# Who rounds h, and what stands inside the modulation block: an edit of one engine's order in a two-layer hybrid trunk

## The chip, the cores and the metric

The kernel runs on 1 core of one Trainium2 chip. The metric is the device time of one launch in microseconds (us), the median of a few runs. Engines are named as in the profile: PE is TensorE (matmul), PEld its weight load, DVE VectorE, ACT ScalarE, POOL GpSimd, SP the engine whose queue issues the transfers.

## The reference, cut to what matters

Two layers of a streaming encoder trunk on 256 positions of width 1024, in fp32. Each layer is a half-step SwiGLU feed-forward, a block of four token mixers, and a second half-step SwiGLU feed-forward, each with a shift, a scale and a gate that come from a vector c:

```
mod = silu(c) @ ada_w[l] + ada_b[l]          # 1024 x 9216 weights a layer
u = x * (1 + scale) + shift
y = (silu(u @ w1) * (u @ w3)) @ w2           # 1024 x 5632 and 2816 x 1024 weights
x = layer_norm(alpha * x + 0.5 * gate * y)
```

The change touches the four feed-forwards. Everything else stands in the reference, but no part of it is edited.

## The kernel before, in words

**Split arithmetic.** Matmuls run on fp32r operands, so each fp32 value is split in two: a high part, the value rounded to fp32r, and a low part, the value less its high part. Each product is three matmuls: high by high, low by high, high by low (L674 to L676 for the way in, L698, L701 and L702 for the way out).

**A feed-forward** is 11 chunks (c = 0 to 10) of 256 hidden columns. A chunk has two hidden tiles of 128 columns (ft = 0 and 1). PE does, for chunk c: 48 matmuls into tile 0, 48 into tile 1, then in most chunks the sum of a modulation block (four small matmuls, or one of 128x512 for a gate), then 24 matmuls out, in the order (rows 0, ft 0), (rows 1, ft 0), (rows 0, ft 1), (rows 1, ft 1). In chunks 9 and 10 it first does only (rows 0, ft 0) and (rows 0, ft 1); chunk 9's other half is done in chunk 10.

**The other engines in chunk c.** ACT: silu of tile 0 (L1782), the high part of w_in for the next chunk's tile 0 (L1789), silu of tile 1, the high part of w_in's tile 1, a gate copy if there is one, the high parts of w_out for the next chunk (L1800). DVE, one instruction after the other in this order: the low parts of both w_out tiles (w_out_low, L1208); for each tile the product h (L1192), its high part by a copy (L1195), its low part (L1197), together ffn_tile, and then the low part of one w_in tile of the next chunk (w_in_low, L1203); then the modulation block. In chunk 0 both w_in_lows come after both tiles. An instruction of DVE that waits holds up all that are behind it in this order.

**The modulation block** (ada_block) is a vector by matrix product done on DVE: 8 steps of 128x512 (L1126 or L1129 first, then 7 of L1132), each of which multiplies one slice of the 2 MB buffer ada_w_sb (part of arena) by a value of silu(c) and adds it to an accumulator. There is one such buffer. SP issues the load of the next block (L346) when the last step of the block before it has counted acc_step. The blocks lie in chunks 0 to 9 of the first two feed-forwards, in chunks 0 to 4 and 7 to 9 of the third, and in 0 and 1 of the fourth. In each chunk SP first issues the next chunk's w_in (2 x 1 MB, L381, freed by PE's first matmul out) and w_out (1 MB, L389, freed by PE's last), then the block's load.

**Chunk 10 of the first and third feed-forward** is written out apart from ffn_chunk on DVE, with the same instructions; in those two feed-forwards some chunks are followed by steps of a rotation table (L1372 to L1378), and the high part of the last w_out waits for the last of these. The names that the change touches are ffn_tile and ffn_chunk of DVE and ffn_chunk of ACT.

Of the kernel before, what the change touches and what calls it, by code (L numbers as in the profile page):

```python
# [32 lines left out]
CHUNKS = D_FF // CW  # L33
# [48 lines left out]
ADA = {(0, 0): dict(zip(range(10), range(0, 10))), (0, 1): dict(zip(range(10), range(12, 22))),  # L82
       (1, 0): dict(zip((0, 1, 2, 3, 4, 7, 8, 9), range(22, 30))), (1, 1): dict(zip((0, 1), (30, 31)))}
# [24 lines left out]
def trunk(nc, x, c, ada_w, ada_b, ln_g, ln_b, ffn_w13, ffn_w2, w_in, w_out, sinks, w_uq, w_iq,  # L108
# [3 lines left out]
    with ctx:  # L112
# [946 lines left out]
        def _(v):  # L1059
# [55 lines left out]
            def ada_block(n, buf, loaded, count, ts=range(8), first=0):  # L1115

                acc = acc_of(n)


                v.wait_ge(sem(loaded), count * 16)  # L1120
                if acc_free(n) and ts[0] == 0:
                    v.wait_ge(sem("ada_summed"), acc_free(n))
                for t in ts:
                    if t == 0 and gate_of(n) is not None:
                        v.wait_ge(sem("gate_bias_loaded"), 16 * (gate_of(n) + 1))
                        v.scalar_tensor_tensor(acc[:, :], buf[:, t - first, :], cs[:, t:t + 1], gate_bias_row[:, :], ALU.mult, ALU.add  # L1126
                                               ).then_inc(sem("acc_step"), 1)
                    elif t == 0:
                        v.tensor_scalar(acc[:, :], buf[:, t - first, :], cs[:, t:t + 1], None, ALU.mult).then_inc(sem("acc_step"), 1)  # L1129
                    else:  # L1130
                        v.wait_ge(sem("acc_step"), n * 8 + t)
                        v.scalar_tensor_tensor(acc[:, :], buf[:, t - first, :], cs[:, t:t + 1], acc[:, :], ALU.mult, ALU.add  # L1132
                                               ).then_inc(sem("acc_step"), 1)
# [50 lines left out]
            def ffn_tile(ft, tile):  # L1184

                v.wait_ge(sem("silu_ready"), tile + (ft + 1))
                gate = PS[:, 5 + 2 * ft, 0:T] if tile % 22 == 0 else PS[:, 4 + ft, T:2 * T]
                ring, parts = h_ring, h_parts
                if tile % 22 == 20:
                    ring, parts = h_ring_last, h_parts_last  # L1190
                    v.wait_ge(sem("acc_step"), 8 * (10, 22, 30, 32)[tile // 22])
                v.tensor_tensor(halves2(ring[:, ft, :]), halves2(silu_ring[:, ft, :]), in_order(gate), ALU.mult  # L1192
                                ).then_inc(sem("h_step"), 1)
                v.wait_ge(sem("h_step"), tile * 2 + (2 * ft + 1))
                v.tensor_copy(parts[:, 2 + ft, :], ring[:, ft, :]).then_inc(sem("h_step"), 1)  # L1195
                v.wait_ge(sem("h_step"), tile * 2 + (2 * ft + 2))
                v.tensor_tensor(parts[:, ft, :], ring[:, ft, :], parts[:, 2 + ft, :].bitcast(F32), ALU.subtract  # L1197
                                ).then_inc(sem("h_done"), 1)

            def w_in_low(slot, ft, tile):  # L1200

                v.wait_ge(sem("w_in_high"), tile + 1)
                v.tensor_tensor(w_in_tile(w_in_lo, slot, ft), w_in_tile(w_in_ring, slot, ft), w_in_hi[ft][:, :, :, :].bitcast(F32),  # L1203
                                ALU.subtract).then_inc(sem("w_in_split"), 1)

            def w_out_low(slot, ft, tile):
                v.wait_ge(sem("w_out_high"), tile + 1)
                v.tensor_tensor(w_out_lo[slot][:, ft, :], w_out_ring[slot][:, ft, :], (w_out_hi_last if tile % 22 >= 20 else w_out_hi)[ft][:, :].bitcast(F32), ALU.subtract  # L1208
                                ).then_inc(sem("w_out_split"), 1)

            def ffn_chunk(l, f, c):

                slot = ff_group(f, c) % 2
                tile = ff_tile(l, f, c)
                by_tile = c == 0
                for ft in range(0 if by_tile else 2):
                    w_out_low(slot, ft, tile + ft)
                for ft in range(2):
                    if by_tile:
                        w_out_low(slot, ft, tile + ft)  # L1220
                    ffn_tile(ft, tile)
                    if c != CHUNKS - 1 and not by_tile:
                        w_in_low(1 - slot, ft, tile + (2 + ft))
                if by_tile:
                    for ft in range(2):
                        w_in_low(1 - slot, ft, tile + (2 + ft))
                if c in ADA[l, f]:
                    n = ADA[l, f][c]
                    ada_block(n, ada_w_sb, "ada_loaded", n + 1 if n < 10 else n - 1)

            def ada_pair(k):

# [511 lines left out]
        def _(a):  # L1744
# [34 lines left out]
            def silu_tile(ft, tile):  # L1779
                a.wait_ge(sem("ag_ready"), tile + (ft + 3))  # L1780
                a.wait_ge(sem("h_done"), tile + (ft + 1))
                a.activation(halves2(silu_ring[:, ft, :]), in_order(PS[:, 4 + (2 * ft if tile % 22 == 0 else ft), 0:T]), ACT.Silu).then_inc(sem("silu_ready"), 1)  # L1782

            def w_in_high(slot, ft, tile):

                a.wait_ge(sem("ag_ready"), tile + 1)
                if tile == 0:
                    a.wait_ge(sem("w_in_loaded0"), in_loads(0, 0))
                a.activation(w_in_hi[ft][:, :, :, :], w_in_tile(w_in_ring, slot, ft), ACT.Copy).then_inc(sem("w_in_high"), 1)  # L1789
# [12 lines left out]
            def ffn_chunk(l, f, c):  # L1802

                last = c == CHUNKS - 1
                slot = ff_group(f, c) % 2
                tile = ff_tile(l, f, c)
                for ft in range(2):
                    silu_tile(ft, tile)
                    if not last:
                        if ft == 0:  # L1810
                            a.wait_ge(sem(f"w_in_loaded{1 - slot}"), in_loads(l, ff_group(f, c + 1)))
                        w_in_high(1 - slot, ft, tile + (2 + ft))
                if not last:
                    if c - 1 in ADA[l, f] and gate_of(ADA[l, f][c - 1]) is not None:
                        copy_gate(ADA[l, f][c - 1])
                    w_out_high(l, f, c + 1)
                elif c - 1 in ADA[l, f] and gate_of(ADA[l, f][c - 1]) is not None:
                    copy_gate(ADA[l, f][c - 1])
# [26 lines left out]
            for l in range(DEPTH):  # L1845
# [171 lines left out]
                else:  # L2017
                    n = l * 3 + 2
# [220 lines left out]
```

## Time and profile before

| what | value |
|---|---|
| median of 3 runs | 1049.12 us (1047.61 to 1053.38) |
| profiled execution | 1054.62 us, its span 1052.8 us |
| PE busy | 1012.4 us, 96% |
| PEld busy | 896.1 us, 85% |
| DVE busy | 884.8 us, 84% |
| ACT busy | 431.5 us, 41% |
| POOL busy | 126.5 us, 12% |
| granted TensorE clock, mean | 0.982 |
| transfers | 250.85 MB, 238 GB/s |

A share is over the whole span. The four feed-forwards are at about 29 to 218, 356 to 534, 547 to 724 and 862 to 1036 us of it; the mixers and the layer norms are between them. All times in the rows below are counted from the start of the span.

### The profile page before, as it was taken

To read this page: it belongs to the slowest core of one execution; us is meant where nothing else is said; L and a number is where in the kernel's file an instruction comes from. 1 tells how busy PE (TensorE), PEld (TensorE's weight loads), DVE (VectorE), ACT (ScalarE), POOL (GpSimd) and SP (SyncE) were. 2 spreads that over 40 slices of the span, in tenths; PEclk is the share of its full clock that TensorE was granted. 3 is DMA by queue.
4 is the path that set the end of the run, shared out by engine and by line. 5 is a ranking of instruction groups with operands and counts; after the bars stand their busy time and mean duration, and the time that the engine had idled before them with its cause. 6 is when DMAs were issued, how large, how long until landed. Compare 5 with 4: busy or idle time off the path is not lost.

```text
span 1052.8 us, 17121 instructions
## 1 busy us (share of the span) xinstructions
PE 1012.4 (96%) x6905; PEld 896.1 (85%) x6905; DVE 884.8 (84%) x1381; ACT 431.5 (41%) x601; POOL 126.5 (12%) x196
## 2 busy tenths in 40 slices
PE   3999999999999999999999999999999999999997
PEld 2899998987875799999999999999787559999995
DVE  6999999978988899999979998997897678766665
ACT  0556433322463444444344643342237244443342
POOL 1015504003000000000000390310300000000000
PEclk9899999989999999999989999999998999999999
DMA  9999999852363689998957995997235247654641
GB/s 344 356 332 346 322 320 333 279 152 80 120 220 121 240 290 329 319 347 315 320 205 251 324 339 178 337 331 217 80 87 174 81 141 267 234 197 166 237 161 40
DMA packets 183882, 250.85 MB, mean 238 GB/s; under 512 B 21676, under 2 KB 131568, under 8 KB 183804
## 3 DMA queue, kind: packets, MB, share of 16 engines
q1 hardware_dynamic: 183804, 249.77, 69.7%
q8 instruction: 55, 0.90, 0.4%
q14 instruction: 23, 0.19, 0.1%
HBM read 248.70 MB, written 1.05 MB: 237 GB/s over the span
## 4 chain that ended last, share of the span: by engine, by line
PE 77%; DVE 12%; DMA 6%; issue 2%; ACT 2%; SPq 1%; POOL 0%; POOLq 0%; DVEq 0%; ACTq 0%
PE PS L676 11%; PE PS L675 11%; PE PS L674 10%; PE PS L797 9%; PE PS L698 5%; PE PS L701 5%; PE PS L702 5%; DMA arena<-in_ada_w_dram 4%; PE PS L882 3%; PE PS L1023 3%; PE PS L804 2%; DVE acc L1132 2%; DVE w_in_lo L1203 2%; DMA xn<-in_ada_w_dram 1%; PE PS L585 1%
## 5 line engine op out<-in xcount | busy, mean ns | idle before, releaser
L674 PE MATMUL PS<-u_hi,w_in_hi 128*128 128x256 f32 x1280 | 352.1, 275 | 0.0
L675 PE MATMUL PS<-u_lo,w_in_hi 128*128 128x256 f32 x1280 | 352.0, 275 | 0.0
L676 PE MATMUL PS<-u_hi,w_in_lo 128*128 128x256 f32 x1280 | 352.0, 275 | 0.0
L674 PEld LDWEIGHTS PS<-u_hi,w_in_hi 128*128 128x128 f32 x1280 | 245.6, 192 | 1.2
L675 PEld LDWEIGHTS PS<-u_lo,w_in_hi 128*128 128x128 f32 x1280 | 245.6, 192 | 1.0
L676 PEld LDWEIGHTS PS<-u_hi,w_in_lo 128*128 128x128 f32 x1280 | 245.8, 192 | 0.0
L1203 DVE TENSOR_TENSOR w_in_lo<-w_in_ring,w_in_hi 128x2048 fp32r<-128x2048 f32 x88 | 201.3, 2294 | 21.8 <-ACT w_in_hi L1789 21.8
L1789 ACT ACTIVATE w_in_hi<-w_in_ring 128x2048 fp32r<-128x2048 f32 x88 | 167.5, 1907 | 6.5 <-DMA w_in_ring<-in_ffn_w_dram 6.4
L1782 ACT ACTIVATE arena<-PS 128x256 f32<-128x256 f32 x88 | 33.7, 384 | 245.1 <-PE PS L676 233.9
L698 PE MATMUL PS<-w_out_hi,h_parts 128*128 128x512 f32 x320 | 127.0, 397 | 3.8 <-DVE h_parts L1197 3.8
L1800 ACT ACTIVATE w_out_hi<-w_out_ring 128x1024 fp32r<-128x1024 f32 x80 | 80.3, 1050 | 118.5 <-PE PS L702 118.5
L701 PE MATMUL PS<-w_out_lo,h_parts 128*128 128x512 f32 x320 | 121.3, 379 | 0.0
L702 PE MATMUL PS<-w_out_hi,h_parts 128*128 128x512 f32 x320 | 121.3, 379 | 0.0
L1208 DVE TENSOR_TENSOR w_out_lo<-w_out_ring,w_out_hi 128x1024 fp32r<-128x1024 f32 x80 | 95.5, 1231 | 9.6 <-ACT w_out_hi L1800 9.6
L1132 DVE SCALAR_TENSOR_TENSOR acc<-arena,cs,acc 128x512 f32<-128x512 f32 x126 | 95.5, 758 | 4.5
L797 PE MATMUL PS<-uT,w_in_ring 128*128 128x256 f32 (+1 forms) x416 | 95.0, 385 | 1.0 <-issue 1.0
L797 PEld LDWEIGHTS PS<-uT,w_in_ring 128*128 128x128 f32 (+1 forms) x416 | 77.7, 190 | 15.7 <-issue 4.7
L698 PEld LDWEIGHTS PS<-w_out_hi,h_parts 128*128 128x128 f32 x320 | 60.5, 189 | 17.7 <-issue 10.3
L1192 DVE TENSOR_TENSOR arena<-arena,PS 128x256 f32<-128x256 f32 x88 | 36.6, 416 | 44.2 <-ACT arena L1782 43.8
L701 PEld LDWEIGHTS PS<-w_out_lo,h_parts 128*128 128x128 f32 x320 | 60.6, 189 | 10.0 <-issue 2.8
L2076 POOL TENSOR_TENSOR rstd<-var_eps,neg_half 128x1 f32<-128x1 f32 x12 | 7.6, 631 | 505.4 <-DVE var_eps L1270 505.4
L702 PEld LDWEIGHTS PS<-w_out_hi,h_parts 128*128 128x128 f32 x320 | 60.5, 189 | 8.6
(343 smaller groups left out, 1368.4 us busy)
## 6 DMA issues: line engine op xcount, KB each, us to landing
w_in_ring<-in_ffn_w_dram SPq DMA_DIRECT2D x88, 1024.0 KB, 7.8
arena<-in_ada_w_dram SPq DMA_DIRECT2D x30, 2048.0 KB, 8.2
w_out_ring<-in_ffn_w_dram SPq DMA_DIRECT2D x44, 1024.0 KB, 7.0
w_in_ring<-in_w_in_dram SPq DMA_DIRECT2D x6, 1024.0 KB, 7.1
w_in_ring<-in_w_in_dram SPq DMA_DIRECT2D x10, 512.0 KB, 5.6
w_out_ring<-in_w_out_dram SPq DMA_DIRECT2D x4, 1024.0 KB, 6.5
w_in_ring<-in_w_in_dram SPq DMA_DIRECT2D x2, 2048.0 KB, 8.8
w_in_ring<-in_w_out_dram SPq DMA_DIRECT2D x4, 1024.0 KB, 6.8
```

The costliest lines, as they stand in the source:

```text
L674: pe.matmul(y, hi, u_moving(u_hi, kt), start=(i == 0), stop=False)
L675: pe.matmul(y, hi, u_moving(u_lo, kt), start=False, stop=False)
L676: mm = pe.matmul(y, lo[:, kt, half, :], u_moving(u_hi, kt), start=False, stop=(i == KT - 1))
L698: mm = pe.matmul(y, h_hi, moving_pairs(his[ft][:, cols]), start=(c == 0 and ft == 0), stop=False)
L701: pe.matmul(y, h_hi, moving_pairs(w_out_lo[slot][:, ft, cols]), start=False, stop=False)
L702: mm = pe.matmul(y, h_lo, moving_pairs(his[ft][:, cols]), start=False, stop=(c == CHUNKS - 1 and ft == 1))
L797: mm = pe.matmul(o[0:w, :], w_in_ring[(G_MIX + m) % 2][:, kt, c0:c0 + w], uT[:, kt, :], start=(i == 0), stop=(i == KT - 1))
L1132: v.scalar_tensor_tensor(acc[:, :], buf[:, t - first, :], cs[:, t:t + 1], acc[:, :], ALU.mult, ALU.add).then_inc(sem("acc_step"), 1)
L1203: v.tensor_tensor(w_in_tile(w_in_lo, slot, ft), w_in_tile(w_in_ring, slot, ft), w_in_hi[ft][:, :, :, :].bitcast(F32), ALU.subtract).then_i ...
L1208: v.tensor_tensor(w_out_lo[slot][:, ft, :], w_out_ring[slot][:, ft, :], (w_out_hi_last if tile % 22 >= 20 else w_out_hi)[ft][:, :].bitcast ...
L1789: a.activation(w_in_hi[ft][:, :, :, :], w_in_tile(w_in_ring, slot, ft), ACT.Copy).then_inc(sem("w_in_high"), 1)
L1800: a.activation((w_out_hi_last if c == CHUNKS - 1 else w_out_hi)[ft][:, :], w_out_ring[slot][:, ft, :], ACT.Copy).then_inc(sem("w_out_high" ...
```

## The change

DVE no longer makes the high part of h in chunks 1 to 9: ACT does (new function h_high), tile 0's after the high part of w_in's tile 0, tile 1's between silu of tile 1 and the high part of w_in's tile 1. In the time between h and its low part (h_low) DVE now does a low weight. In these chunks the low part of w_in's tile 0 is made in two halves (w_in_low_half). The low part of w_in's tile 1 moves from ahead of the modulation block to behind its third step. In chunk 10 of the second and fourth feed-forward, each w_out_low now stands just ahead of its own tile. Chunk 0, and chunk 10 of the other two, are as before. No PE or SP instruction changes.

```diff
                 v.tensor_tensor(halves2(ring[:, ft, :]), halves2(silu_ring[:, ft, :]), in_order(gate), ALU.mult
                                 ).then_inc(sem("h_step"), 1)
+                if 2 <= tile % 22 < 20:
+                    return
                 v.wait_ge(sem("h_step"), tile * 2 + (2 * ft + 1))
                 v.tensor_copy(parts[:, 2 + ft, :], ring[:, ft, :]).then_inc(sem("h_step"), 1)
+                h_low(ft, tile, ring, parts)
+
+            def w_in_low_half(slot, ft, tile, half):
+                kts = slice(4 * half, 4 * half + 4)
+                v.wait_ge(sem("w_in_high"), tile + 1)
+                ins = v.tensor_tensor(w_in_tile(w_in_lo, slot, ft)[:, kts], w_in_tile(w_in_ring, slot, ft)[:, kts],
+                                      w_in_hi[ft][:, kts, :, :].bitcast(F32), ALU.subtract)
...
-                for ft in range(0 if by_tile else 2):
-                    w_out_low(slot, ft, tile + ft)
-                for ft in range(2):
-                    if by_tile:
-                        w_out_low(slot, ft, tile + ft)
-                    ffn_tile(ft, tile)
-                    if c != CHUNKS - 1 and not by_tile:
-                        w_in_low(1 - slot, ft, tile + (2 + ft))
...
-                if c in ADA[l, f]:
-                    n = ADA[l, f][c]
-                    ada_block(n, ada_w_sb, "ada_loaded", n + 1 if n < 10 else n - 1)
...
+                w_out_low(slot, 0, tile)
+                ffn_tile(0, tile)
+                w_out_low(slot, 1, tile + 1)
+                h_low(0, tile)
+                w_in_low_half(1 - slot, 0, tile + 2, 0)
+                ffn_tile(1, tile)
+                w_in_low_half(1 - slot, 0, tile + 2, 1)
+                h_low(1, tile)
+                if n is not None:
+                    ada_block(n, ada_w_sb, "ada_loaded", loaded, range(3))
+                w_in_low(1 - slot, 1, tile + 3)
+                if n is not None:
+                    ada_block(n, ada_w_sb, "ada_loaded", loaded, range(3, 8))
...
+            def h_high(ft, tile):
+                a.wait_ge(sem("h_step"), tile * 2 + (2 * ft + 1))
+                a.activation(h_parts[:, 2 + ft, :], h_ring[:, ft, :], ACT.Copy).then_inc(sem("h_step"), 1)
...
                         if ft == 0:
                             a.wait_ge(sem(f"w_in_loaded{1 - slot}"), in_loads(l, ff_group(f, c + 1)))
-                        w_in_high(1 - slot, ft, tile + (2 + ft))
+                            w_in_high(1 - slot, ft, tile + (2 + ft))
+                        if c:
+                            h_high(ft, tile)
+                        if ft == 1:
+                            w_in_high(1 - slot, ft, tile + (2 + ft))
```

## Rows read from the trace of the kernel before

**Rows 1.** The page: busy time by engine; the chain that ended last, by engine.
```profile
PE 1012.4 (96%) x6905; PEld 896.1 (85%) x6905; DVE 884.8 (84%) x1381; ACT 431.5 (41%) x601; POOL 126.5 (12%) x196
PE 77%; DVE 12%; DMA 6%; issue 2%; ACT 2%; SPq 1%; POOL 0%; POOLq 0%; DVEq 0%; ACTq 0%
```

**Rows 2.** Stretches of one chunk each: length, then busy time and count by engine.
```profile
422.90:438.80 15.90, 15.90 (x121) 15.26 (x120) 14.62 (x19) 6.38 (x6) 0.00 (x0) 1.00 0.94 327
929.22:945.12 15.90, 15.90 (x121) 15.26 (x120) 9.70 (x11) 6.38 (x6) 0.00 (x0) 1.00 0.57 198
```

**Rows 3.** Waits of PE: us in total, times, the longest.
```profile
PE PS L698 <- DVE h_parts L1197: 3.8, 9, 0.7
PE PS L698 <- DVE h_parts_last L1197: 3.1, 3, 2.3
```

**Rows 4.** DVE in order of time, second feed-forward, chunk 4 (starts 438.80).
```profile
446.87 0.29 DVE L1195 CAST h_parts<-arena 128x256 fp32r<-128x256 f32 x1
451.94 2.29 DVE L1203 TENSOR_TENSOR w_in_lo<-w_in_ring,w_in_hi 128x2048 fp32r<-128x2048 f32 x1 [0.59 <-ACT w_in_hi L1789]
454.14 0.48 DVE L1129 TENSOR_SCALAR arena<-arena,cs 128x512 f32<-128x512 f32 x1
454.66 5.48 DVE L1132 SCALAR_TENSOR_TENSOR arena<-arena,cs 128x512 f32<-128x512 f32 x7
460.06 1.22 DVE L1208 TENSOR_TENSOR w_out_lo<-w_out_ring,w_out_hi 128x1024 fp32r<-128x1024 f32 x1
```

**Rows 5.** Issues of the modulation loads by SP, and their time to landing (us).
```profile
444.26 0.55 SPq L346 DMA_DIRECT2D arena<-in_ada_w_dram  x1
460.17 0.55 SPq L346 DMA_DIRECT2D arena<-in_ada_w_dram  x1
DMA to landing us min/median/max: 8.1/8.2/15.4
```

**Rows 6.** The first and the last of nine such issues in three feed-forwards; of four in the third.
```profile
59.42 0.55 SPq L346 DMA_DIRECT2D arena<-in_ada_w_dram  x1
189.82 0.55 SPq L346 DMA_DIRECT2D arena<-in_ada_w_dram  x1
...
380.73 0.55 SPq L346 DMA_DIRECT2D arena<-in_ada_w_dram  x1
508.72 0.55 SPq L346 DMA_DIRECT2D arena<-in_ada_w_dram  x1
...
570.42 0.55 SPq L346 DMA_DIRECT2D arena<-in_ada_w_dram  x1
618.14 0.55 SPq L346 DMA_DIRECT2D arena<-in_ada_w_dram  x1
```

**Rows 7.** The chain that ended last: its two longest waits for these loads.
```profile
138.95 11.16 DMA arena<-in_ada_w_dram
172.89 10.88 DMA arena<-in_ada_w_dram
```

**Rows 8.** DVE: blocks that waited for their load; what follows the first feed-forward's last block.
```profile
68.81 0.75 DVE L1126 SCALAR_TENSOR_TENSOR acc<-arena,cs,gate_bias_row 128x512 f32<-128x512 f32 x1 [0.51 <-DMA arena<-in_ada_w_dram]
69.61 5.48 DVE L1132 SCALAR_TENSOR_TENSOR acc<-arena,cs,acc 128x512 f32<-128x512 f32 x7
...
205.74 0.68 DVE L1372 TENSOR_TENSOR rot_flat<-sin_t,cos_t 128x512 f32<-128x512 f32 x1
...
579.91 0.49 DVE L1129 TENSOR_SCALAR qk_tanh<-arena,cs 128x512 f32<-128x512 f32 x1 [0.61 <-DMA arena<-in_ada_w_dram]
```

**Rows 9.** Around tile 1 of chunk 9 of the last feed-forward: DVE and PE.
```profile
1020.05 0.42 DVE L1192 TENSOR_TENSOR arena<-arena,PS 128x256 f32<-128x256 f32 x1 [1.26 <-ACT arena L1782]
1020.84 0.43 DVE L1197 TENSOR_TENSOR h_parts<-arena,h_parts 128x256 fp32r<-128x256 f32 x1
1021.41 0.45 PE L698 MATMUL PS<-w_out_hi,h_parts 128*128 128x512 f32 x1 [0.51 <-DVE h_parts L1197]
```

**Rows 10.** An ACT group: instruction, count, busy us, mean ns, idle before.
```profile
L1759 ACT ACTIVATE u_hi<-uT_lo 128x256 fp32r<-128x256 f32 x12 | 5.0, 417 | 0.4
```

More of the change, by code:

```diff
@@ L1193, in ffn_tile, with h_low @@
                                 ).then_inc(sem("h_step"), 1)
+                if 2 <= tile % 22 < 20:
+                    return
                 v.wait_ge(sem("h_step"), tile * 2 + (2 * ft + 1))
                 v.tensor_copy(parts[:, 2 + ft, :], ring[:, ft, :]).then_inc(sem("h_step"), 1)
+                h_low(ft, tile, ring, parts)
+            def h_low(ft, tile, ring=h_ring, parts=h_parts):
                 v.wait_ge(sem("h_step"), tile * 2 + (2 * ft + 2))
@@ L1198, in ffn_tile @@
                                 ).then_inc(sem("h_done"), 1)
+            def w_in_low_half(slot, ft, tile, half):
[3 more added lines that the diff above has]
+                                      w_in_hi[ft][:, kts, :, :].bitcast(F32), ALU.subtract)
+                if half == 1:
+                    ins.then_inc(sem("w_in_split"), 1)
             def w_in_low(slot, ft, tile):
@@ L1214, in ffn_chunk @@
                 tile = ff_tile(l, f, c)
-                by_tile = c == 0
-                for ft in range(0 if by_tile else 2):
-                    w_out_low(slot, ft, tile + ft)
-                for ft in range(2):
-                    if by_tile:
-                        w_out_low(slot, ft, tile + ft)
-                    ffn_tile(ft, tile)
-                    if c != CHUNKS - 1 and not by_tile:
-                        w_in_low(1 - slot, ft, tile + (2 + ft))
-                if by_tile:
-                    for ft in range(2):
-                        w_in_low(1 - slot, ft, tile + (2 + ft))
-                if c in ADA[l, f]:
-                    n = ADA[l, f][c]
-                    ada_block(n, ada_w_sb, "ada_loaded", n + 1 if n < 10 else n - 1)
+                n = ADA[l, f].get(c)
+                loaded = None if n is None else n + 1 if n < 10 else n - 1
+                if c in (0, CHUNKS - 1):
+                    for ft in range(2):
+                        w_out_low(slot, ft, tile + ft)
+                        ffn_tile(ft, tile)
+                    if c == 0:
+                        for ft in range(2):
+                            w_in_low(1 - slot, ft, tile + (2 + ft))
+                    if n is not None:
+                        ada_block(n, ada_w_sb, "ada_loaded", loaded)
+                    return
+                w_out_low(slot, 0, tile)
[9 more added lines that the diff above has]
+                w_in_low(1 - slot, 1, tile + 3)
+                if n is not None:
+                    ada_block(n, ada_w_sb, "ada_loaded", loaded, range(3, 8))
             def ada_pair(k):
```

## The prediction, on record before the changed kernel ran

> **What bounds the kernel now.** First the page's busy times and chain [rows 1]: PE is busy for 1012.4 of 1052.8 us and is 77% of the chain that ended last. The rest of the chain is mostly DVE (12%) and DMA (6%), so there are stretches that PE does not set. Then stretches of one chunk [rows 2]: where nothing delays PE, a chunk takes 15.90 us and PE is busy in all of it. No edit of DVE or ACT can make such a chunk shorter. In the second feed-forward DVE is busy for 14.62 us of the chunk, in the last one 9.70. Then PE's waits [rows 3]: all that PE loses to h is 3.8 us in nine waits and 3.1 in three. Their sum, 6.9 us or 0.7% of the span, is about all that this change can win.
>
> Last the loop between the modulation block and its load. There is one buffer, so the next load is issued when the last step is done (460.14; issue 460.17), and the next block can't start before it lands, 8.2 us later in the median [rows 4, 5]. In chunk 4 of the second feed-forward: issued 444.26, landed by 452.5, while DVE comes to the block at 454.14, after w_in_low of tile 1. The landing had 1.7 us to spare and nobody saw the load. In the first feed-forward the spare time is sometimes gone: two loads of 11.16 and 10.88 us stand in the chain that ended last [rows 7], and DVE waited 0.51 us before the block at 68.81 [rows 8]. There the loop is on the path that sets the end: its last block is followed by the rotation table, for which the last high w_out waits, and PE waits 2.3 us for h behind that [rows 3].
>
> **The change part by part.**
>
> *The copy of h leaves DVE.* It removes two copies of 0.29 us and a step of 0.04 each [rows 4], 0.66 us a chunk. ACT pays 0.42 us for the same shape [rows 10], twice a chunk; it is busy 6.38 of 15.90 us [rows 2], so this is hidden unless a tile waits for it. Cutting one w_in_low in two costs one more overlap of 0.08 us. DVE has 0.58 us less to do in each of 36 chunks. Where DVE is not on the path this is worth nothing.
>
> *h is low-rounded later.* In chunk 9 tile 1's product starts at 1020.05, its low part ends at 1021.27 and PE goes on at 1021.41 [rows 9]: 1.22 us on DVE, 0.14 to PE. Now half a w_in_low (1.22, the size of a w_out_low [rows 4]) stands between them: 0.42 + 1.14 + 0.35 = 1.91 us. (Each instruction starts 0.08 before its predecessor ends.) ACT's 0.42 fits under the half. So the low part of tile 1 is 0.7 us later where DVE was on time. In chunk 9 PE already waits, so it loses 0.7 more; that is so in three feed-forwards, and not in the first, where DVE is late. In chunks 1 to 8 PE asks for tile 1 six matmuls of 512 columns later. A chunk is 96 of 256 and 24 of 512 columns, 144 units in 15.90 us, so six are 1.33 us. Of these 0.5 to 0.67 were already used up, which leaves 0.66 to 0.8 against 0.7: nothing to 0.06 us a chunk. I take 0.06.
>
> *The fillers.* From the end of a block DVE now needs four pieces of 1.14, two of 0.34 and two of 0.35, 5.94 us, until tile 1's low part. PE wants it 13.3 us after the chunk's start (96 + 24 of the 144 units) less 0.15. So a block may end 7.2 us into the next chunk, later only where PE also sums a block. In [rows 4] it ended at 5.4: slack 1.8.
>
> *The low w_in moves into the block.* It is the same instruction, but before it stood ahead of the wait for the load, and filled the time until the landing. Now DVE comes to the wait 2.2 + 0.6 us earlier, finds the load not landed (1.7 us spare before), idles, and then does the low weight between landing and last step, which releases the next load. It lengthens the loop by 2.29 less 0.08 twice less the gap of 0.03 that it fills, 2.10 us. The block itself is 5.99 us (454.14 to 460.14), a gate's 6.26 (68.81 to 75.09) [rows 4, 8]. A round is now load + 0.06 + block + 2.10: with 8.2 us 16.35, with a gate 16.6, where PE's chunk is 15.90. Queued behind the wait are the rest of the block, tile 1's low w_in, and the whole next chunk of h; behind the last step waits SP with the next load. No queue of SP changes its order.
>
> The rule "Overlap DMA with compute" of the Trainium skill (DMA: Bandwidth & Descriptors, Rules for kernel authors) asks for an early issue and a late wait. Here the wait is made earlier and the next issue later. By that rule the edit is a loss; these rows agree as far as the 1.7 us go that were spare.
>
> **The sum.** In each feed-forward the rounds between two issues [rows 6] are set against the new ones.
>
> First: eight rounds took 189.82 - 59.42 = 130.4. New: eight loads of 8.2 and the known excess (9.4 by the block at 68.81, 11.16, 10.88: +6.9) are 72.5; 8 x 2.16 = 17.3; three gates and five others 48.7. That is 138.5, +8.1, and the last round 16.35 against 16.0 (205.82) makes +8.4. The two 11 us loads were slow because three others were under way; at a slower pace they should be quicker, at most by 5.7 in all. I take 1.5, so **+7.0**, all on the path. Bounds +2 to +10.
>
> Second: eight rounds took 128.0. New 8 x 10.36 + 48.7 = 131.6, +3.6 (3.3 with the 8.16 that most have). PE had about 1.8 of slack, but the two residual steps in chunks 2 and 8 (1.2 us each on DVE) stand in it, and chunk 9 adds up to 0.7. **+2.2**, bounds 0 to 4.
>
> Third: three rounds took 47.7. New 3 x 10.36 + 18.5 = 49.6, and the first load took 9.5 (570.42 to 579.91 [rows 6, 8]); a second one like it makes 52.2, +4.5. Blocks pause after chunk 4, with some 2.2 of slack there: +1.8; a PE wait of 0.65 in chunk 8 goes, chunks 9 and 10 add 1.1. **+2.2**, bounds 0 to 5.
>
> Fourth: only two blocks. 0.7 in chunk 9 and six times 0.06: **+1.1**, bounds 0 to 2.
>
> Together +12.5. Against the profiled execution's own 1054.62 us that is 1067.1. That execution lies 5.5 above the median of the runs; on the median, 1049.12 + 12.5 = **1061.6 us**. The bounds add up to +2 and +21.
>
> **The rivals.**
>
> *The relief wins (faster).* If the landings come before DVE does, the loop never closes, and DVE's 0.58 us a chunk is what counts: 9 x 0.58 = 5.2 us on the first feed-forward's path, where DVE and not the load stands most often, and PE's waits of 3.8 us [rows 3] go too, less 2.1 for chunk 9: some -5, 1044. For it: PE waits for h in twelve places, and ACT is 41% busy. [...] Against it: with DVE 2.8 us earlier at the wait and 1.7 spare, a load would have to take under 8.2 + 1.7 - 2.8 = 7.1 us, and the least is 8.1 [rows 5]. Its point of decision is a landing ahead of DVE. Chance 7%.
>
> *Given back (little change).* The loop is longer, but loads of the first feed-forward fall to 8.2 us when the pace slackens, and the others have enough slack: +2 there, +0.5 to +1.5 in each other one: +3 to +6, 1052 to 1055. For it: 5.7 us of excess in two loads. Chance 20%.
>
> *Loads stretch.* Each load now starts some 1.5 us later in its chunk and meets the 2 MB of w_in that follow PE's first matmul out; the transfer engines are 94% busy in the chunk of [rows 2]. At 9.4 us instead of 8.2 for 20 of the 27 loads: 24 us more on the loop, half of it hidden by slack: 1070 to 1078. The same sign has ACT's copy of tile 0, which stands behind a w_in_high that may wait for its own load. Chance 15%.
>
> **How the numbers follow.** The forecast has 58%. Its own range is 1056 to 1068. My 80% range is 1052 to 1070: it takes in most of the second rival and leaves out the first and most of the third. Less than 0.5% (5.2 us) can't be told from no change with a kernel of this spread. Faster by more: part of the first rival, 5%. Within: the rest of it, half of the second and a tail of the forecast, 15%. Slower: 80%.
>
> **What would show it.** Right: in the first three feed-forwards DVE idles before nearly every block for its load, 0.5 to 2 us (now 0.51 and 0.61, [rows 8]); issues of L346 lie 16.3 or 16.6 us apart or more, never 15.9; the low part of w_in tile 1 stands behind three steps, with the fourth step some 2.1 us after the third; the chain that ended last holds far more of DMA than 6%; PE's waits for h grow, the longest at the end of the first feed-forward; in the last feed-forward only chunk 9 is longer, with a wait of 1.2 to 1.4. Wrong: if DVE still comes to the blocks after the landings, or if the rounds of the first feed-forward stay at 16.3 on average.

## The result, and the profile after

The changed kernel is slower: 1065.49 us in the median (1063.79 to 1067.31) against 1048.55 (1047.61 to 1053.38) for the kernel before, a ratio of 1.0157 with a 95% interval of 1.0138 to 1.0177. That is 16.9 us. The forecast was 1061.6, so the sign and the range (1052 to 1070) held, and the size was 3.9 us short.

The page of the changed kernel, its busy times and its chain by engine, answers to [rows 1]:

```profile
PE 1015.1 (95%) x6905; PEld 892.1 (84%) x6905; DVE 859.1 (81%) x1345; ACT 459.5 (43%) x673; POOL 116.5 (11%) x196
PE 53%; DMA 19%; DVE 18%; issue 6%; ACT 1%; SPq 1%; POOL 0%; POOLq 0%; DVEq 0%; ACTq 0%
```

DVE has 25.7 us less to do, in 36 instructions less (0.58 us in each of 36 chunks, 20.9 us, had been worked out), and the program takes longer. PE's share of the chain fell from 77 to 53%, DMA's rose from 6 to 19%.

Now the modulation loads: the view of the one line that issues them, with who waited for them (us, times). First the kernel before:

```profile
  DVE acc L1126: 1.9, 3
  DVE qk_tanh L1129: 0.6, 1
```

The same view of the kernel after:

```profile
  DVE acc L1126: 11.2, 6
  DVE acc L1129: 8.4, 6
  DVE qk_tanh L1129: 7.7, 5
  DVE arena L1129: 3.9, 2
  DVE sig_o L1129: 1.4, 2
...
DMA to landing us min/median/max: 8.0/8.3/15.5
```

Four blocks waited 2.5 us in all before, 21 waited 32.6 us after. Three more blocks, each for a gate, waited for the small bias row that is issued right behind their load and landed 0.1 to 0.3 us after it:

```profile
DVE acc L1126 <- DMA gate_bias_row<-in_ada_b_dram: 6.7, 3, 2.4
```

So 24 of the 30 blocks waited, 39.3 us in all. The loads are as fast as they were: 8.3 us in the median against 8.2 [rows 5].

DVE in order of time in the second feed-forward, from the end of chunk 4 (it starts at 430.14) into chunk 5 (446.17); the loop that [rows 4] showed for the kernel before:

```profile
442.94 0.42 DVE L1203 TENSOR_TENSOR h_parts<-arena,h_parts 128x256 fp32r<-128x256 f32 x1
445.02 0.48 DVE L1129 TENSOR_SCALAR qk_tanh<-arena,cs 128x512 f32<-128x512 f32 x1 [1.66 <-DMA arena<-in_ada_w_dram]
445.54 1.54 DVE L1132 SCALAR_TENSOR_TENSOR qk_tanh<-arena,cs,qk_tanh 128x512 f32<-128x512 f32 x2
446.99 2.28 DVE L1218 TENSOR_TENSOR w_in_lo<-w_in_ring,w_in_hi 128x2048 fp32r<-128x2048 f32 x1
449.19 3.89 DVE L1132 SCALAR_TENSOR_TENSOR qk_tanh<-arena,cs,qk_tanh 128x512 f32<-128x512 f32 x5
453.00 1.22 DVE L1223 TENSOR_TENSOR w_out_lo<-w_out_ring,w_out_hi 128x1024 fp32r<-128x1024 f32 x1
```

SP's issues on either side of it:

```profile
436.48 0.55 SPq L346 DMA_DIRECT2D arena<-in_ada_w_dram  x1
453.12 0.55 SPq L346 DMA_DIRECT2D arena<-in_ada_w_dram  x1
```

Issued 436.48, landed after 8.51 us, first step at 445.02, last step done at 453.09, next issue 453.12: a round of 16.64 us. DVE idles for 1.66 us in front of the block, where the low weight stood before.

Stretches of one chunk each, as in [rows 2]: a plain one of the second feed-forward, chunk 2 of the third, a plain one and chunk 9 of the last:

```profile
446.17:462.21 16.04, 16.04 (x122) 15.18 (x120) 13.54 (x18) 7.21 (x8) 0.00 (x0) 1.00 0.90 310
586.55:606.45 19.90, 17.91 (x122) 16.60 (x121) 17.65 (x22) 10.07 (x12) 4.68 (x11) 0.91 0.93 320
956.49:972.52 16.03, 16.03 (x121) 15.17 (x120) 9.58 (x11) 7.10 (x8) 0.00 (x0) 1.00 0.58 197
1020.63:1035.37 14.74, 13.54 (x109) 12.91 (x108) 7.24 (x10) 7.83 (x9) 0.00 (x0) 1.00 0.55 204
```

And the waits of PE for h [rows 3], with one of ACT (us in total, times, longest):

```profile
PE PS L698 <- DVE h_parts L1203: 10.5, 9, 2.0
ACT s5p L1887 <- DVE prm L1420: 9.3, 2, 4.8
PE PS L698 <- DVE h_parts_last L1203: 4.9, 3, 3.4
```

PE's 6.9 us became 15.4.

**The ledger.** A feed-forward is measured from PE's first matmul of chunk 1 to DVE's first gated product behind chunk 10. Each kernel was profiled twice ("again" is a second profile, described below); all in us. The last column is the time at a granted clock of 0.5 (half of full speed), inside and outside the four feed-forwards:

| | 1st | 2nd | 3rd | 4th | sum | rest of span | at clock 0.5: inside, outside |
|---|---|---|---|---|---|---|---|
| before | 165.45 | 158.69 | 158.66 | 156.69 | 639.50 | 413.33 | 3.4, 34.1 |
| before again | 164.26 | 158.69 | 158.20 | 156.69 | 637.84 | 407.25 | 3.2, 19.7 |
| after | 171.98 | 162.75 | 162.58 | 158.19 | 655.50 | 409.93 | 9.6, 26.1 |
| after again | 169.90 | 160.86 | 162.44 | 158.20 | 651.39 | 405.86 | 6.8, 17.7 |
| forecast of the difference | +7.0 | +2.2 | +2.2 | +1.1 | +12.5 | 0 | |

The first pair differs by +6.5, +4.1, +3.9 and +1.5, in all 16.0; the second by +5.6, +2.2, +4.2 and +1.5, in all 13.5. The spans of the first pair differ by 12.6 only, since outside the feed-forwards the kernel before had 34.1 us at the lower clock and the changed one 26.1. The mixers and the norms, which nobody edited, take 406 to 413 us in these four profiles. Less half of their time at the lower clock they take 396.3, 397.4, 396.9 and 397.0, so nearly all of that spread is the clock.

### The profile page after: what moved, and what is told of

Same layout as the page of the kernel before. It is cut to its first block, busy times and chain, and to the rows that moved or that the text cites. A ratio compares the mean times of both kernels' runs of the same rounds, so it can differ in the third digit from the quotient of the medians.

```text
span 1065.4 us, 17183 instructions
## 1 busy us (share of the span) xinstructions
PE 1015.1 (95%) x6905; PEld 892.1 (84%) x6905; DVE 859.1 (81%) x1345; ACT 459.5 (43%) x673; POOL 116.5 (11%) x196
## 4 chain that ended last, share of the span: by engine, by line
PE 53%; DMA 19%; DVE 18%; issue 6%; ACT 1%; SPq 1%; POOL 0%; POOLq 0%; DVEq 0%; ACTq 0%
DMA arena<-in_ada_w_dram 16%; PE PS L797 9%; DVE acc L1132 6%; PE PS L676 5%; PE PS L675 5%; PE PS L674 5%; PE PS L698 3%; PE PS L701 3%; PE PS L702 3%; PE PS L882 3%; PE PS L1023 3%; DVE qk_tanh L1132 3%; PE PS L804 2%; DVE arena L1132 2%; DVE sig_o L1132 2%
## 5 line engine op out<-in xcount | busy, mean ns | idle before, releaser
L1218 DVE TENSOR_TENSOR w_in_lo<-w_in_ring,w_in_hi 128x2048 fp32r<-128x2048 f32 x52 | 118.6, 2290 | 9.5 <-ACT w_in_hi L1819 9.5
L1223 DVE TENSOR_TENSOR w_out_lo<-w_out_ring,w_out_hi 128x1024 fp32r<-128x1024 f32 x80 | 98.2, 1227 | 4.6 <-ACT w_out_hi L1830 4.6
L797 PEld LDWEIGHTS PS<-uT,w_in_ring 128*128 128x128 f32 (+1 forms) x416 | 77.0, 188 | 15.4 <-issue 4.7
L1210 DVE TENSOR_TENSOR w_in_lo<-w_in_ring,w_in_hi 128x1024 fp32r<-128x1024 f32 x72 | 88.5, 1229 | 0.0
```

Source lines behind the costliest of these rows:

```text
L797: mm = pe.matmul(o[0:w, :], w_in_ring[(G_MIX + m) % 2][:, kt, c0:c0 + w], uT[:, kt, :], start=(i == 0), stop=(i == KT - 1))
L1210: ins = v.tensor_tensor(w_in_tile(w_in_lo, slot, ft)[:, kts], w_in_tile(w_in_ring, slot, ft)[:, kts], w_in_hi[ft][:, kts, :, :].bitcast(F3 ...
```

## The experiments

### The second half of the edit: the low weight out of the block, and nothing else

**e1_low_first** is the changed kernel with tile 1's low w_in back ahead of the block; ACT's copies and the two halves stay.

```diff
-                    ada_block(n, ada_w_sb, "ada_loaded", loaded, range(3))
                 w_in_low(1 - slot, 1, tile + 3)
                 if n is not None:
-                    ada_block(n, ada_w_sb, "ada_loaded", loaded, range(3, 8))
+                    ada_block(n, ada_w_sb, "ada_loaded", loaded)
```

> The changed kernel with one thing put back: the low part of w_in's tile 1 is made ahead of the whole modulation block again; the copies of h stay on ScalarE and the half weight stays between product and low part. Theory (the loop load, block, load is what costs): the low weight fills the time to the landing again, DVE's blocks take 6.0 or 6.3 us from the first step to the last instead of 8.1 or 8.3, rounds between issues of the modulation loads fall from 16.2 to 17.9 back to 15.9 in plain chunks, and some 12 of the 17 us come back: 1050 to 1055 us against 1048.6 of before. What stays: chunk 9 and 0.14 us a chunk in the last feed-forward, where nothing but h's detour acts. Rival (the detour of h over ScalarE is what costs): at least 1060 us, rounds as in the changed kernel.

1055.35 us, ratio 1.008 (1.0065 to 1.0095), just above the 1050 to 1055 expected. No block waits for its load any more: the view of the issuing line lists nobody who waited. In order of time on DVE, the load is there when the low weight ends:

```profile
438.07 2.29 DVE L1218 TENSOR_TENSOR w_in_lo<-w_in_ring,w_in_hi 128x2048 fp32r<-128x2048 f32 x1 [0.81 <-ACT w_in_hi L1817]
440.28 0.48 DVE L1129 TENSOR_SCALAR qk_tanh<-arena,cs 128x512 f32<-128x512 f32 x1
440.79 5.48 DVE L1132 SCALAR_TENSOR_TENSOR qk_tanh<-arena,cs,qk_tanh 128x512 f32<-128x512 f32 x7
```

Half of the loss goes with this one instruction's place. The other half is not the loop. In the ledger's stretches e1 is 5.5 us above the mean of the two profiles of the kernel before (644.2 against 638.7).

**e2_move_alone** is the converse: the kernel before, with that one instruction moved behind the third step (`inside` is true in chunks 1 to 9).

```diff
-                    if c != CHUNKS - 1 and not by_tile:
+                    if c != CHUNKS - 1 and not by_tile and ft == 0:
                         w_in_low(1 - slot, ft, tile + (2 + ft))
...
+                    ada_block(n, ada_w_sb, "ada_loaded", loaded, range(3 if inside else 8))
+                if inside:
+                    w_in_low(1 - slot, 1, tile + 3)
+                if n is not None and inside:
+                    ada_block(n, ada_w_sb, "ada_loaded", loaded, range(3, 8))
```

> The kernel before with one edit alone: in chunks 1 to 9 the low part of w_in's tile 1 moves behind the third step of the modulation block; h is still rounded on DVE, no weight is halved. Theory of the loop: blocks take 8.1 or 8.3 us, DVE waits for most landings (by 0 to 1 us, as it comes 2.2 us earlier than before with 1.2 to 2.4 spare), rounds of 16.3 to 16.9, the first feed-forward ends 4 to 8 us later, the whole 1056 to 1062 us; the last feed-forward is as before. Rival (the detour costs): below 1051 us.

1062.3 us, ratio 1.0151 (1.013 to 1.0172): nearly the whole loss, 0.3 us above the range expected. PE's waits for h grow to 15.7 us (12.0, and 3.7 at the ends of feed-forwards), and the blocks wait for their loads 23 times, 26.3 us, the other three for a gate's bias, 4.5 us:

```profile
PE PS L698 <- DVE h_parts L1197: 12.0, 19, 1.3
DVE acc L1126 <- DMA arena<-in_ada_w_dram: 10.0, 6, 4.1
DVE qk_tanh L1129 <- DMA arena<-in_ada_w_dram: 8.2, 6, 2.7
```

So the move alone costs 1.5%, the rest alone 0.8%, both together 1.6%. In the time they don't add (14.8 and 7.9 us against 16.9). In the ledger's stretches they come nearer to it: e2 adds 12.0 us (650.7), e1 5.5, in all 17.5, where the changed kernel adds 16.0 and 13.5. That a waiting round hides some of the other delay would fit, but it is not shown.

### Open the loop instead: half loads

**e4_split_load** leaves DVE's order as changed and cuts each modulation load in two of 1 MB. The first half is issued when the fourth step of the block before is done (in chunks 1 to 9), and DVE waits for the second one only at its fifth step (t = 4).

```diff
-                if n:
-                    sp.wait_ge(sem("acc_step"), n * 8)
...
+                for half in range(2):
+                    if n:
+                        sp.wait_ge(sem("acc_step"), n * 8 - (4 if half == 0 and early else 0))
...
+                    if loaded == "ada_loaded" and t == max(4, ts[0]):
+                        v.wait_ge(sem("ada_first_loaded0"), 32 + count * 16)
```

> The changed kernel with each 2 MB modulation load issued as two of 1 MB in chunks 1 to 9: the first half as soon as the fourth step of the block before has read it, the second after the eighth; DVE waits for the second half only at its fifth step. The order of DVE and ScalarE is the changed kernel's. Theory of the loop: a half lands in 5 to 7 us, needed 5 to 11 us after its issue, so the loop no longer closes: DVE's waits for landings before blocks shrink to a few us in all, rounds are 15.9 in plain chunks, and most of the loss comes back: 1050 to 1056 us. Rival (DVE's order or h's detour costs, not the load): above 1061 us.

1049.0 us, ratio 1.0022 (1.0004 to 1.004), better than the 1050 to 1056 expected. No block waits for a landing. The loads (count, size, median us to landing), then PE's waits:

```profile
arena<-in_ada_w_dram SPq DMA_DIRECT2D x60, 1024.0 KB, 7.8
```

```profile
PE PS L701 <- DVE h_parts_last L1208: 3.2, 3, 2.2
PE PS L701 <- DVE h_parts L1208: 3.0, 4, 1.2
```

The low weight still stands inside the block and costs next to nothing once the load doesn't wait for the block's last step. That settles the mechanism: not the instruction's place as such, but what it does to the release of the buffer. PE's waits are back at 6.2 us. The fair partner of e4 is the kernel before with the same half loads (e6_before_split_load, below): against it the four feed-forwards of e4 are longer by 1.2, 1.0, 0.1 and 1.5 us (639.7 against 636.0). These 3.7 us are what the detour of h costs without the loop.

### Is it chunk 2, and is it ACT's copy there?

In the third feed-forward one chunk alone, chunk 2, holds 3.4 of the 3.9 us (16.53 became 19.90). The first theory was that ACT's copy of h is late there, as it stands behind a high weight, and that 1.5 to 2.5 us would come back. **e3_chunk2_dve** gives the copy back to DVE in chunk 2 of each feed-forward.

```diff
-                if 2 <= tile % 22 < 20:
+                if 2 <= tile % 22 < 20 and tile % 22 // 2 != 2:
                     return
...
-                        if c:
+                        if c and c != 2:
                             h_high(ft, tile)
```

> The changed kernel, but in chunk 2 of each feed-forward DVE makes the high part of h itself. In the first and third feed-forward ScalarE waits in chunk 2 for the parameters that DVE copies after chunk 1's block, and loads activation tables, so silu of tile 0 is late, and the copy of h stands behind a 1.9 us high weight after it: PE waits 2.2 us there in the third. Theory: in the third feed-forward, where the block loop ends after chunk 4 with 2 us of slack, this wait is on the path, chunk 2 falls from 19.9 to about 17.7 us and the whole is 1.5 to 2.5 us faster than the changed kernel's 1065.5; in the first, chunk 2 is shorter too but the loop takes it back by the end. Rival (all of the loss is the loop): no difference, 1065 to 1066.

1065.0 us, ratio 1.0161 (1.0143 to 1.0179): no gain, a miss. The chunk, and ACT's wait in it:

```profile
588.93:607.77 18.84, 16.46 (x122) 15.34 (x121) 16.81 (x24) 9.37 (x10) 4.53 (x11) 1.00 0.91 311
```

```profile
597.29 0.44 ACT L1888 ACTIVATE s5p<-log_dt 64x8 f32<-64x8 f32 x2 [4.82 <-DVE prm L1421]
```

The chunk is 1.1 us shorter, but not by the edit: PE is busy for 16.46 us in it at a granted clock of 1.00, where it was busy for 17.91 at 0.91; its wait grew from 2.0 to 2.4. DVE starts tile 0's low part 12.35 us into the chunk, the changed kernel 12.39, since the low weight of w_out's tile 1 stands ahead of it in either. What hardly moved is what comes before: ACT waits 4.8 us for a small copy named prm, which DVE makes behind the block of chunk 1. In the changed kernel, ACT in order of time:

```profile
588.81 1.28 ACT L1887 ACT_TABLE_LOAD   x1
594.53 0.44 ACT L1887 ACTIVATE s5p<-log_dt 64x8 f32<-64x8 f32 x2 [4.44 <-DVE prm L1420]
594.98 1.28 ACT L1807 ACT_TABLE_LOAD   x1
596.28 0.38 ACT L1807 ACTIVATE arena<-PS 128x256 f32<-128x256 f32 x1
596.69 1.91 ACT L1819 ACTIVATE w_in_hi<-w_in_ring 128x2048 fp32r<-128x2048 f32 x1
598.51 0.40 ACT L1812 ACTIVATE h_parts<-arena 128x256 fp32r<-128x256 f32 x1
```

and where it ends, on PE:

```profile
599.51 0.67 PE L698 MATMUL PS<-w_out_hi,h_parts 128*128 128x512 f32 x1 [1.99 <-DVE h_parts L1203]
```

Read down: the block of chunk 1 ends late, so prm is copied late (594.25, which is 7.70 us into the chunk, against 5.88 before). Only then can ACT do its exponentials, load silu's table again, do silu, a high weight, and at last tile 0's copy of h, for which DVE and PE wait. DVE's product of tile 0 starts 10.14 us into the chunk, before 8.33, and its low part 12.39, before 9.11: of 3.3 us, 1.8 are there at the product, and 1.5 come between product and low part. Of chunk 2's 3.4 us, then, 1.7 are PE's wait (0.3 before, 2.0 after) and 1.7 its busy time (16.22 before, 17.91 after), most of that the clock that fell in it (16.46 at clock 1.00 in e3).

**e8_parameters_early** tests this second theory. It puts the copy prm ahead of the last five steps of the block of chunk 1, and changes nothing else.

```diff
                 w_in_low(1 - slot, 1, tile + 3)
+                if f == 0 and c == 1:
+                    v.wait_ge(sem("prm_turned"), l + 1)
+                    v.tensor_copy(prm[:, :], PS[:, 7, 0:ROWS]).then_inc(sem("prm_ready"), 1)
                 if n is not None:
...
-                    if c == 1:
-                        v.wait_ge(sem("prm_turned"), l + 1)
-                        v.tensor_copy(prm[:, :], PS[:, 7, 0:ROWS]).then_inc(sem("prm_ready"), 1)
```

> The changed kernel, but in the first and third feed-forward the copy of the parameters from PSUM, which stands behind chunk 1's modulation block, is made inside it, behind the low weight and ahead of the fourth step. e3_chunk2_dve left chunk 2 of the third feed-forward at 18.8 us with ScalarE waiting 4.8 us for this copy. Theory (the longer block delays the copy, ScalarE's exponential, two table loads and silu behind it): the wait falls to under 1 us, chunk 2 of the third feed-forward from 19.9 to 17.5 or less, of the first from 19.0 to 17.5 or less. In the third the 2 to 3 us stay gained to the end, since its loop has slack; in the first most is taken back by the loop by chunk 10. The whole: 2 to 4 us faster than the changed kernel in the same call. Rival (the loop is the bound in the third too): its length from chunk 1 to the end stays at 162 to 163 us.

Beside it ran the changed kernel itself, **a1_after_again**.

> The changed kernel unchanged, on the same chip as e8_parameters_early, to compare the two and to see how its executions differ: 1063 to 1067 us, the four feed-forwards from chunk 1 to the end 171 to 172, 162 to 163, 161 to 163 and 158.2 us as in its first profile; the rest, mixers and layer norms, within 4 us by the stretches at half clock.

1061.07 us against 1063.19; ratios to the kernel before 1.0125 (1.01 to 1.015) and 1.0149 (1.0122 to 1.0176). The intervals overlap, so the time does not show a gain. The traces show what happened in the chunk. The chunk, then ACT's waits:

```profile
586.90:604.57 17.67, 16.46 (x123) 15.34 (x121) 14.39 (x19) 10.31 (x12) 6.84 (x11) 1.00 0.85 293
```

```profile
ACT s5p L1887 <- DVE prm L1255: 3.9, 2, 2.2
```

In the changed kernel's second profile the chunk took 20.01 us and those two waits were 8.6 us; here 17.67 and 3.9 (less than 1 us each and 17.5 had been expected). PE waits 1.1 us in the chunk instead of 2.1, and the clock stays at 1.00, where both profiles of the changed kernel have a piece at the lower clock. The third feed-forward fell from 162.44 to 160.78, so the late parameters are 1.7 of its 4.2 us in that pair, part of it by way of the clock. In the first feed-forward nothing is won: chunk 2 takes 18.21 us there as in the changed kernel's second profile (18.20), and the whole of it 172.54 against 169.90, with two loads of 10.34 and 10.38 us where the other had 8.38 and 9.86. The four together are 652.3 against 651.4.

### The half of a low weight between the product and its low part

**e5_low_first_half_last** starts from e1_low_first and moves the second half of tile 0's low w_in behind the low part of h.

```diff
                 ffn_tile(1, tile)
-                w_in_low_half(1 - slot, 0, tile + 2, 1)
                 h_low(1, tile)
+                w_in_low_half(1 - slot, 0, tile + 2, 1)
```

> As e1_low_first (low w_in of tile 1 ahead of the block), and the second half weight of tile 0 moves from between product and low part of h's tile 1 to behind the low part. h's high part stays on ScalarE. Theory (product to low part of tile 1 takes 1.9 us because the half stands between): it falls to about 1.35, chunks of 16.04 us go back to 15.90 and chunk 9 from 14.74 to 14.2: 34 x 0.14 + 3 x 0.55 is 5 to 6 us less than e1_low_first, so 1048 to 1051 against 1047.5 of before. Rival (ScalarE's rounding itself costs, by its place behind the high weight): 1053 us or more.

1050.12 us, ratio 1.0026 (1.0008 to 1.0045). A plain chunk and chunk 9 of the last feed-forward, in its windows:

```profile
435.11:451.01 15.90, 15.90 (x122) 15.26 (x121) 14.02 (x18) 7.23 (x8) 0.00 (x0) 1.00 0.95 332
1000.95:1015.13 14.18, 13.55 (x110) 12.91 (x108) 6.91 (x10) 7.27 (x9) 0.00 (x0) 1.00 0.60 217
```

The plain chunk is back at 15.90, chunk 9 at 14.18 (14.06 before, 14.74 after). The half weight that was meant to fill the time between product and low part was what held tile 1 up: the four feed-forwards fall from 644.2 in e1 to 639.1.

DVE is no earlier at its block for all that. In the chunk shown above (it starts at 435.11), ACT's copy of tile 1 waits for DVE's product, and the high weight of w_in's tile 1 stands behind the copy; DVE waits for both in turn. ACT, then DVE in order of time, then DVE's waits for the copies over the whole program:

```profile
446.90 0.42 ACT L1810 ACTIVATE h_parts<-arena 128x256 fp32r<-128x256 f32 x1 [0.49 <-DVE arena L1192]
447.22 1.90 ACT L1817 ACTIVATE w_in_hi<-w_in_ring 128x2048 fp32r<-128x2048 f32 x1
447.35 0.43 DVE L1203 TENSOR_TENSOR h_parts<-arena,h_parts 128x256 fp32r<-128x256 f32 x1 [0.48 <-ACT h_parts L1810]
449.15 2.29 DVE L1218 TENSOR_TENSOR w_in_lo<-w_in_ring,w_in_hi 128x2048 fp32r<-128x2048 f32 x1 [0.25 <-ACT w_in_hi L1817]
DVE h_parts L1203 <- ACT h_parts L1810: 24.7, 49, 0.9
```

The low weight of tile 1 starts 14.04 us into the chunk, where it started 13.14 us into it before (451.94 in a chunk from 438.80 [rows 4]). DVE is busy for 20.1 us less over the program than before, but it waits 24.7 us for the copies, and in such a chunk the block starts 0.9 us later than before. This is a further cost of the detour, and e5 keeps it.

### Was there anything to win?

**b0_before_again** is a second profile of the kernel before.

> The kernel before, unchanged, in another execution, to see where its own executions differ: the profiled one took 1054.6 us, the timed ones 1044.6 to 1050.4. If it is the granted clock, the feed-forward chunks have the same lengths to 0.1 us (15.90 in plain chunks) and the difference lies in the mixers and layer norms, with another count of stretches at clock 0.5 (34 us in all in the first profile). If the modulation loads differ, the first feed-forward's chunks 6 to 10 differ by some us.

1046.87 us, span 1045.1: 7.7 us less than its first profile, with the feed-forwards 1.7 shorter and the unedited rest 6.1.

**e6_before_split_load** is the kernel before with the half loads of e4_split_load, the same diff.

> The kernel before with each modulation load in chunks 1 to 9 as two of 1 MB, the first half issued when the fourth step has read it. No order on DVE or ScalarE changes. Theory: the three blocks of the first feed-forward that waited for a landing (chunks 1, 6, 8: 0.5, 1.2 and about 1 us) no longer do, and the waits of PE in its chunks 7 and 10 shrink: 1 to 3 us faster than before, 1044.5 to 1046.5. Rival (DVE's own work is the bound there, or more transfers in flight slow w_in): no change or slower, 1047 to 1050.

1048.67 us, ratio 1.001 (0.9992 to 1.0027), a miss. The first feed-forward is the shortest seen (162.28), the others are as before (158.76, 158.24, 156.74), and the time shows nothing.

**e7_split_relief** adds ACT's copies except in chunk 2, with the half weight behind the low part: the relief of DVE without the loop, without the half weight in h's way and without the late copy in chunk 2. Its main lines against e6:

```diff
+                h_low(0, tile)
+                w_in_low_half(1 - slot, 0, tile + 2, 0)
+                ffn_tile(1, tile)
+                h_low(1, tile)
+                w_in_low_half(1 - slot, 0, tile + 2, 1)
+                w_in_low(1 - slot, 1, tile + 3)
+                if n is not None:
+                    ada_block(n, ada_w_sb, "ada_loaded", loaded)
```

> All that the theory calls good: split loads, h's high part on ScalarE but not in chunk 2, low w_in of tile 1 ahead of the block, second half weight behind the low part of h. Theory: DVE has 0.6 us less a chunk, no block waits for its load, PE's chunks are 15.90 but for chunk 9: 2 to 4 us faster than before, 1043.5 to 1045.5. Rival (ScalarE's rounding costs as much as it relieves): not faster than e6_before_split_load.

1049.74 us, ratio 1.0023 (1.0004 to 1.0041), another miss: no version beats the kernel before. PE's 15.90 us a chunk are the floor. PE's waits for h, 6.9 and 5.9 us in the two profiles of the kernel before, are 5.4 in e6, 6.5 in e7 and 7.3 in e5. In e7 those within the chunks fell to 1.4, but the longest, at the end of the first feed-forward, grew to 3.8, for the reason seen in e5: DVE waits 20.4 us for ACT's copies, and its blocks start 0.9 us later in a plain chunk, the one ahead of the rotation table 1.2 us (16.54 us into its chunk, 15.39 in e6).

Part of what was won was lost to the clock. The mean granted clock was 0.986 over the twelve runs of e6 and of e7 each, and 0.989 over the 29 runs of the kernel before beside them. A span times its mean granted clock is an estimate of what it would take at the full clock. It gives 1032.8 for e6, 1033.3 for e7 and 1034.7 for the kernel before. Why the clock was lower is not shown.

## Why the forecast held, and where it was short

**The loop.** The prediction's central step was a block 2.10 us longer between landing and next issue. Measured, from the first step to the end of the last: 8.07 us for a plain block and 8.34 for a gate's, against 5.99 and 6.26, so 2.08. Of the 26 blocks in chunks 1 to 9, 20 start 0.02 or 0.03 us after their landing, and 3 more within 0.3. Rounds are 16.1 to 18.2 us, but for one of 21.7 in the third feed-forward that was 21.6 before; none is 15.90, and the least is a little under the 16.3 that was to be the least. (The waits named for the kernel before, 0.51 and 0.61 us, left out one of 1.22 us at 150.13.) e1, e2 and e4 show from three sides that this is the cause of the larger part.

**First feed-forward: +7.0, measured +6.5 and +5.6.** Issues ran from 59.63 to 195.54, 135.9 us instead of 130.4, where 138.5 was worked out. The loads gave back more than the 1.5 us assumed: nine took 81.6 us before and 77.2 after, 4.4 less; the two of 11.16 and 10.88 [rows 7] became 8.43 and 9.74. Against that the block in chunk 7, which took 6.98 us before, took 9.05, 0.7 more than the 8.36 in the sum. The last block's end was 6.0 us later (the rotation table at 211.77, before 205.74 [rows 8]), and PE's wait behind it grew from 2.3 to 3.4:

```profile
211.77 0.68 DVE L1397 TENSOR_TENSOR rot_flat<-sin_t,cos_t 128x512 f32<-128x512 f32 x1
...
219.19 0.77 PE L698 MATMUL PS<-w_out_hi_last,h_parts_last 128*128 128x512 f32 x1 [3.42 <-DVE h_parts_last L1203]
```

**Second: +2.2, measured +4.1 and +2.2.** The first profile had a first load of 9.76 us, and chunk 2 took 18.43; in the second, chunk 2 took 16.91. The rival "loads stretch" is here in one load, not in twenty.

**Third: +2.2, measured +3.9 and +4.2.** This is the term whose content was wrong, not just its size. The prediction let the slack of chunks 1 and 2 take the delay, and had DVE's queue behind the wait as the block, a low weight and the next h. It left out prm, which stands behind that block and which ACT and its table waited for. [Rows 8] shows the first half of it, a block at 579.91 that waited; what is queued behind the block was not followed. e8 puts 1.7 us on it, a part of which is the clock, which no term of the sum had.

**Fourth: +1.1, measured +1.5 both times.** There is no loop in most of it, so it shows the h edit by itself: six plain chunks at 0.14 instead of the 0.06 taken (the sign "only chunk 9 is longer" did not hold), and chunk 9 at +0.68, where 0.70 was worked out from [rows 9]. Around tile 1 of that chunk, DVE and PE:

```profile
1031.96 0.42 DVE L1192 TENSOR_TENSOR arena<-arena,PS 128x256 f32<-128x256 f32 x1 [1.69 <-ACT arena L1807]
1032.30 1.22 DVE L1210 TENSOR_TENSOR w_in_lo<-w_in_ring,w_in_hi 128x1024 fp32r<-128x1024 f32 x1
1033.44 0.42 DVE L1203 TENSOR_TENSOR h_parts<-arena,h_parts 128x256 fp32r<-128x256 f32 x1
1034.00 0.45 PE L698 MATMUL PS<-w_out_hi,h_parts 128*128 128x512 f32 x1 [1.19 <-DVE h_parts L1203]
```

Product, half weight, low part, and PE waits 1.19 us, as forecast (1.2 to 1.4). The 0.08 us by which the plain chunks were undersized is small, but it falls on all 15 chunks that took 16.04 us, 1.2 us in all. The bound of the slack had been "0.5 to 0.67 already used up"; it was a little more.

**The rivals.** "The relief wins" needed landings ahead of DVE. Three blocks of 26 had one, by 0.4 to 0.8 us, all in the third feed-forward, and nothing was won there. e5 and e7, where landings do come ahead, aren't faster either. So the rival would have failed even with its condition met: DVE's time went into waits for ACT's copies, and its blocks came 0.9 us later. The prediction had ACT's copies hidden "unless a tile waits for it", and put no price on the high weight of tile 1 that stands behind the copy. (Its own terms, -5.2, -3.8 and +2.1, add up to -6.9 and not to "some -5"; nothing else hangs on that.) The Trainium skill (Perfetto Trace Analysis, Optimizing Scalar/DVE Operations) says that offloading to Scalar may make sense if DVE is saturated. DVE was busy for 14.62 of 15.90 us in such a chunk [rows 2], and after 0.6 us had been taken off (14.02 in e5) the chunk still took 15.90: here DVE's busy share is not the bound, as PE is. "Given back" was right in its part for the first feed-forward (4.4 us of loads) and wrong in that this was enough.

**Luck.** The clock hides how well the terms fit. If each us at the lower clock is taken to cost half a us (an estimate), the feed-forwards grew by 5.1, 4.1, 2.2 and 1.5 us in the first pair and by 5.5, 2.2, 2.5 and 1.5 in the second, in all 12.9 and 11.7, against 7.0, 2.2, 2.2, 1.1 and 12.5. The sum is so near because the first feed-forward was put too high (its loads gave back more) and the others mostly too low. The third's number then agrees by luck: what filled it was the late parameters, which were not in it.

**What stays open.** The time grew by 16.9 us, and by 14.4 in the runs of a1_after_again (1063.19 against 1048.84), where the feed-forwards grew by 16.0 and 13.5. In the latter runs the mean granted clock was 0.985 for the changed kernel and 0.989 for the kernel before, so some 3 to 4 of the 14.4 us go with the clock (an estimate: 0.003 to 0.004 of 1060). That is the term the sum lacked. Why a changed kernel gets the lower clock for longer is not shown. e5 and e7 have feed-forwards as long as the kernel before (639.05 and 638.44, between its 637.84 and 639.50), and yet 2.4 to 2.7 us more time. Their mean granted clocks are 0.987 and 0.986 against 0.989, and the spans times these 1035.1 and 1033.3 against 1034.7, so the clock accounts for most of that.

## What to carry to other kernels

Before an instruction is put inside a stretch that holds a single buffer, work out the round: load, wait, the whole hold time, next issue. What the round has to spare against the pace of the bounding engine is used up first, here 1.7 of 2.10 us; what goes beyond it is paid once a round (16.3 to 16.6 us instead of 15.90), and load times that vary are then paid as well. Splitting the load took that away here. Follow what is queued behind the moved instruction to its end on the other engines, small copies and table loads too. When work goes to an idle engine, look at what stands behind it there: here a high weight came 0.9 us later for it. A filler between a product and its low part is free only as long as the consumer asks later than the filler ends.

## What the runs showed of the hardware

- A 2 MB modulation load took 7.9 us at the least in the two profiles of the kernel before and 8.0 in those of the changed one, with medians of 8.2 to 8.5; a 1 MB half of it took 7.8 us in the median in e4. The halves gain by their earlier issue, not by their size.
- A table load on ACT took 1.28 us each time, and one exponential between two silus costs two of them. The Trainium skill (ScalarE: Activation LUTs, What ACT_TABLE_LOAD costs) gives about 1283 ns for it, and the trace agrees.
- The granted clock fell to half, 1.2 GHz, for 20.6 to 39.0 us in all of a profiled execution. One such piece came at 599.6, right behind PE's wait of 1.99 us in chunk 2 of the third feed-forward, and one at the same place in the second profile, 1.1 us behind a wait of 2.10. It made PE's busy time in the chunk 17.9 us instead of 16.5. In e3 PE waited 1.9 and 0.5 us in that chunk, and the clock did not fall, so the wait alone does not explain it. The two profiles of the kernel before, 37.5 and 22.9 us at the lower clock, have spans 7.7 us apart.
